# Sample query products moved between gated tiles, page numbers read once, and the order of the SP queue, in a hybrid decoder layer

## The chip, the core and the metric

The kernel runs on one core of a Trainium2 chip. The engines of the core run on their own and meet at semaphores: PE (TensorE) multiplies, with its weight loads (PEld) beside it; DVE (VectorE), ACT (ScalarE) and POOL (GpSimd) work elementwise; SP (SyncE) issues nearly all transfers between HBM and SBUF, one after the other, from a program of its own, and its rows are named SPq in the profile. The metric is the device time of one launch in microseconds (us). Spans and stretches below are counted from the first instruction of the profiled execution.

## The reference, cut to what matters

One layer for 1,024 prompt rows and 32 sample rows (8 requests of 4 tokens). It has a first feed-forward half step, a mixing step, an output projection, a second feed-forward half step and a gated embedding. The change touches the mixing step:

```python
def token_mix(n, prm, q_pos, attend, conv_hist):
    z = n @ prm['w_in']
    cq, ckv_raw, kpe_raw, u = z[..., :o1], z[..., o1:o2], z[..., o2:o3], z[..., o3:]
    q = jnp.einsum('btr,rhd->bthd', rmsnorm(cq, prm['g_q']), prm['w_q_up'])
    q_nope = q[..., :QK_NOPE]
    q_pe = rope(q[..., QK_NOPE:], q_pos)
    ckv = rmsnorm(ckv_raw, prm['g_kv'])
    kpe = rope(kpe_raw, q_pos)
    att = attend(q_nope, q_pe, ckv, kpe)
    v = u[..., :CONV_CH] * jax.nn.sigmoid(u[..., CONV_CH:])     # gated tiles
    ...                                                         # depthwise convolution, 31 taps

def sample_attention(q_nope, q_pe, q_pos, ckv_all, kpe_all, w_uk, w_uv):
    q_abs = jnp.einsum('bthn,rhn->bthr', q_nope, w_uk)
    s = (jnp.einsum('bthr,bsr->bhts', q_abs, ckv_all)
         + jnp.einsum('bthp,bsp->bhts', q_pe, kpe_all))
    ...
    pr = jax.nn.softmax(s, axis=-1).astype(ckv_all.dtype)
    o_lat = jnp.einsum('bhts,bsr->bthr', pr, ckv_all)
    return jnp.einsum('bthr,rhv->bthv', o_lat, w_uv).reshape(B, T, H * V_HEAD)
```

For the prompt rows the keys and values are the 1,024 rows themselves. For the sample rows they are 2,048 cached rows in pages of 128, found through a page table, plus the 4 new ones.

## The kernel before

All 1,056 rows are held as columns, cut into three blocks of 352. The large products are split into three fp32r products (`split_product`, L467 to L471: `wlo` by `n_hi`, `whi` by `n_lo`, `whi` by `n_hi`), so a tile of one 128-wide weight block and 352 columns takes 8 x 3 matmuls. Weight tiles stream from HBM into `raw`, are split by ACT into `whi` and by DVE into `wlo`, and sit in a ring of six.

**The gated tiles** (L581 to L589) are the last part of the input projection. There are 4 channel chunks `c` by 3 row blocks `r`, twelve in all, each with 48 matmuls into two PSUM banks. For each one ACT applies the sigmoid (`gate`, L1003 to L1007) and DVE multiplies (`glu`, L1456 to L1461). Between the first ones PE sums squares for the norms of the latents `cq` and `ckv`.

**The sample queries** (L592 to L616) follow all twelve tiles on PE. 24 products of 128x32 (48 matmul rows in the trace, since an fp32 product is two passes) of `sw` and the sample columns of `cq` go to bank 7. DVE scales them into `qs` (L1500). 32 further products of `qs` with `sw` and `ident` (64 rows) absorb the key up-projection; ACT copies the result into `qabs` (L1044). Between the two, PE transposes the 32 new latent rows, which DVE copies into `ckvnew`, and DVE makes `newT` and the rotary rows of `k` (L1509 to L1511).

**The attention** (L665 to L778) runs over four pairs of heads, `p` = 0 to 3. In each pair PE makes the pair's queries, keys and values out of `cq` and `ckv` with the pair's weights `pw` (`proj`, z = 0 to 7, L671 and L699), then goes through eight blocks of prompt rows: scores (L714), transposes of the probabilities (L729), values (L739), and at the end the reciprocals of the sums (L749). Into it are woven four tiles of sample attention per pair, n = 4p to 4p + 3, sixteen in all, each for 256 cached rows of four requests: `sample_scores(n)` (L629) reads `ttile[n % 2]`, `sample_probs_T(n)` (L643) transposes, `sample_values(n)` (L655) reads `ctile[n % 2]`. The first stands behind z = 2, the second behind the scores of block 1, the third behind block 2 and the fourth in block 5. DVE and POOL share the convolution: POOL takes its chunks in one run once all gated tiles are done, and DVE puts one tap (`convolve`, L1525) behind most of its steps.

**The queue of SP** is written out by hand. After the weight tiles it holds the stores of `kpe` and `ckv`, then, once the last gated tile is multiplied, the loads of `tab` and `pw`, then `load_t(0)`, `load_c(0)`, `load_t(1)`, `load_c(1)`, then five stores of the convolution's state (L375, L377), and then for n = 2 to 15 `load_t(n)`, `load_c(n)`, with the next pair's `pw` behind every fourth. `load_t(n)` may start when `sample_scores(n - 2)` is done, `load_c(n)` when `sample_values(n - 2)` is. Each is eight transfers, one per page and request, and each transfer is preceded by a read of its page number from SBUF into a register:

```python
    def load_t(eng, n):
        if n >= BUFS:
            eng.wait_ge(ss_ready, n - BUFS + 1)
        for j, pg, page in pages_of(eng, n):
            eng.dma_start(ttile[n % BUFS][:, j, :, pg * PAGE:(pg + 1) * PAGE], cacheT[page]).then_inc(t_in[n % BUFS], 16)
```

`pages_of` is a generator, so the read of one page number (L322) and its transfer (L329 or L336) alternate. `ttile1` and `ctile0` lie where `sw` and `qs` lay, `ttile0` where `cs` and `tabs` lay, and `tab`, `pw`, `q`, `k` and `V` lie over `raw` and the ring of weight tiles. PE then goes on to the output projection and the rest of the layer.

Of the kernel before, what the change touches and what calls it, by code (L numbers as in the profile page):

```python
# [6 lines left out]
P = 128  # L7
D_MODEL, SEQ, DEC_B, DEC_T = 1024, 1024, 8, 4
ROWS = SEQ + DEC_B * DEC_T
NRB = 3  # L10
# [112 lines left out]
def program(nc, wstream, pairw, xT, hist, gains, trig, qtrig, strig, samplew, ident_d, tri_d, smask_d, cache, cacheT,  # L123
# [82 lines left out]
    z1 = scope()  # L206
    wuv = sb(z1, "wuv", [P, VC, HEADS * VH])
    z1.close()
    pw = sb(zc, "pw", [P, PW])
    z1 = scope()  # L210
    olatT = sb(z1, "olatT", [P, VC, 2, P])
    z1.close()
    q = sb(zc, "q", [P, 2, SEQ])
# [102 lines left out]
    def pages_of(eng, n):  # L316

        grp, c = divmod(n, TILES)
        for j in range(4):
            for pg in range(PPT):  # L320
                at = (4 * grp + j) * N_PAGES + PPT * c + pg
                yield j, pg, eng.value_load(ptab[0:1, at:at + 1], min_val=0, max_val=cache.shape[0] - 1)  # L322

    def load_t(eng, n):

        if n >= BUFS:
            eng.wait_ge(ss_ready, n - BUFS + 1)
        for j, pg, page in pages_of(eng, n):
            eng.dma_start(ttile[n % BUFS][:, j, :, pg * PAGE:(pg + 1) * PAGE], cacheT[page]).then_inc(t_in[n % BUFS], 16)  # L329

    def load_c(eng, n):

        if n >= BUFS:
            eng.wait_ge(c_used, n - BUFS + 1)
        for j, pg, page in pages_of(eng, n):
            eng.dma_start(ctile[n % BUFS][:, j, pg, :], cache[page]).then_inc(c_in[n % BUFS], 16)  # L336
# [5 lines left out]
    def _(sp):  # L342
# [16 lines left out]
        sp.wait_ge(const_in, 4 * 16)  # L359
        sp.wait_ge(kpe_roped, 1)  # L360
        sp.dma_start(kpeT, kpe[:, :]).then_inc(kpe_out, 16)
        sp.wait_ge(lat_norm, 2 * NRB)
        sp.dma_start(ckvT, ckv[:, :, :]).then_inc(out_state, 16)
        sp.wait_ge(pair_ready, T_FF2)
        sp.dma_start(tab[:, :], qtrig).then_inc(trig_in, 16)
        sp.dma_start(pw[:, :], pairw[0]).then_inc(pw_in, 16)
        sp.wait_ge(qs_ready, 1)
        load_t(sp, 0)
        sp.wait_ge(qa_made, 1)
        load_c(sp, 0)  # L370
        load_t(sp, 1)
        load_c(sp, 1)
        sp.wait_ge(hist_in, 16 * CC)
        sp.wait_ge(pair_free, 2 + T_FF2)
        sp.dma_start(convp, vext[:, :, SEQ:SEQ + HIST]).then_inc(out_state, 16)  # L375
        for c in range(CC):
            sp.dma_start(convs[:, c], vs[:, c, :, DEC_T:DEC_T + HIST]).then_inc(out_state, 16)  # L377
        for n in range(BUFS, LAST + 1):
            load_t(sp, n)
            load_c(sp, n)  # L380
            if n % STEPS == 2:
                p = n // STEPS + 1
                sp.wait_ge(proj_ready, Z_PROJ * p)
                if p < PAIRS:
                    sp.dma_start(pw[:, :], pairw[p]).then_inc(pw_in, 16)
                else:
                    sp.dma_start(wuv[:, :, :], wuv_d).then_inc(wuv_in, 16)
# [78 lines left out]
    def _(pe):  # L466
# [110 lines left out]
        y = Y_LAT  # L577
        for c in range(CC):
            for r in range(NRB):
                t = T_WIN + c * NRB + r  # L580
                pe.wait_ge(w_split, N_WIN + 6 + 2 * c + 2)  # L581
                pe.wait_ge(pair_free, t + 1)
                b = 2 * (t % 2)
                contract(ps[:, b, 0:RB], (2 * c) % RING, r)
                contract(ps[:, b + 1, 0:RB], (2 * c + 1) % RING, r).then_inc(pair_ready, 1)
                x = c * NRB + r - 2
                if 0 <= x < 2 * NRB:
                    row_sum(y, lat_red, x + 1, sqs[:, 0, :])
                    y += 1  # L589


        pe.wait_ge(const_in, 4 * 16)  # L592
        pe.wait_ge(sw_in, 3 * 16)
        pe.wait_ge(lat_norm, 2 * NRB)
        for hd in range(HEADS):
            for c in range(QC):
                w0 = hd % 2 * QC * P + c * P
                last = nc.tensor.matmul(ps[:, 7, hd * NEW:(hd + 1) * NEW], sw[:, hd // 2, w0:w0 + P], cq[:, c, SEQ:ROWS],
                                        start=(c == 0), stop=(c == QC - 1))
        last.then_inc(qs_made, 1)  # L600
        for c in range(VC):
            last = nc.tensor.transpose(ps[0:NEW, 6, c * P:(c + 1) * P], ckv[:, c, SEQ:ROWS],
                                       ident[:, 0:P])
        last.then_inc(new_made, 1)
        pe.wait_ge(qs_ready, 1)
        pe.wait_ge(pair_free, 2 + T_FF2)
        for hd in range(HEADS):
            for c in range(C96 + 1):
                m = ROPE if c == C96 else min(K96, KV_RANK - c * K96)
                out = ps[0:m, hd // 4, (hd % 4 * 4 + c) * NEW:(hd % 4 * 4 + c + 1) * NEW]  # L610
                if c == C96:
                    last = nc.tensor.matmul(out, ident[NOPE:P, P:P + ROPE], qs[NOPE:P, hd, :], start=True, stop=True)
                else:
                    w0 = SW_UKT + hd % 2 * KV_RANK + c * K96
                    last = nc.tensor.matmul(out, sw[0:NOPE, hd // 2, w0:w0 + m], qs[0:NOPE, hd, :], start=True, stop=True)
        last.then_inc(qa_made, 1)  # L616
# [47 lines left out]
        for p in range(PAIRS):  # L664
# [10 lines left out]
            for z in range(4):  # L675
                hh, s0 = z // 2, z % 2 * 512
                if z == 2:
                    pe.wait_ge(new_ready, 1)
                    pe.wait_ge(av_out, QB * p + 1)
# [75 lines left out]
            if p == 0:  # L755
                pe.wait_ge(qabs_ready, 1)
# [118 lines left out]
    def _(act):  # L875
# [147 lines left out]
        lat_squares(0, 0)  # L1023
        for x in range(CC * NRB):
            gate(*divmod(x, NRB))
# [12 lines left out]
        act.wait_ge(qa_made, 1)  # L1038
        for b in range(2):
            for c in range(C96 + 1):  # L1040
                m = ROPE if c == C96 else min(K96, KV_RANK - c * K96)
                dst = qabs[NOPE:K96, 2] if c == C96 else qabs[0:m, c]
                src = ps[0:m, b, :].rearrange("p (h s n) -> p h s n", h=4, s=4)[:, :, c, :]
                last = nc.scalar.activation(dst[:, :, 4 * DEC_T * b:4 * DEC_T * (b + 1)]  # L1044
                                            .rearrange("p b (h t) -> p h b t", h=4),
                                            src.rearrange("p h (b t) -> p h b t", b=DEC_B), ACT.Copy)
        last.then_inc(qabs_ready, 1)

# [10 lines left out]
        def sample_exp(n):  # L1059
# [4 lines left out]
            else:  # L1064
                act.wait_ge(kpe_out, 16)
                act.wait_ge(kpe_ready, 1)
            if n >= 2:
# [178 lines left out]
    def _(ve):  # L1246
# [240 lines left out]
        for x in range(CC * NRB):  # L1487
# [8 lines left out]
            if x == 2 * NRB + 2:  # L1496
                rope_keys()

        ve.wait_ge(qs_made, 1)
        nc.vector.scalar_tensor_tensor(out=qs[:, :, :], in0=ps[:, 7, 0:HEADS * NEW].rearrange("p (h n) -> p h n", h=HEADS),  # L1500
                                       scalar=SCALE, in1=tabs[:, :].rearrange("p (o n) -> p o n", o=1)
                                       .broadcast_to([P, HEADS, NEW]), op0=ALU.mult, op1=ALU.mult).then_inc(qs_ready, 1)
        ve.wait_ge(new_made, 1)
        nc.vector.tensor_copy(ckvnew[:, :], ps[0:NEW, 6, 0:KV_RANK]).then_inc(new_ready, 1)
# [384 lines left out]
```

## Time and profile before

| | us |
|---|---|
| median of 3 runs | 2373.71 (2373.28 to 2376.27) |
| the profiled execution | 2374.75 |
| its span, first to last instruction | 2372.9 |
| PE busy | 2235.9 (94%) |
| DVE, ACT, POOL busy | 1236.1, 599.9, 308.4 |
| mean granted clock of TensorE | 0.975 |

The page's slices show PE at 9 tenths nearly everywhere but in the slices from about 960 to 1340 us, the attention, where it stands at 5 to 9 and the granted clock dips. Stretches of the trace are therefore read one by one. The rows of a timeline give the start, the busy time, the engine, the line, what is written and read, and in brackets how long the engine was idle before and who ended it. A busy PE is not PE at its peak: the column of the granted clock (1.00 is 2.4 GHz, 0.50 is 1.2 GHz) says at which of its two levels it ran.

### The profile page before, as it was taken

The numbers are of one execution on the slowest core, as the hardware profiler recorded it, in microseconds if no ns is written. First come the engines' busy times: TensorE is split into PE (matmuls) and PEld (weight loads), VectorE is DVE, ScalarE is ACT, GpSimd is POOL, SyncE is SP. The second block draws the span as 40 slices with busy tenths as digits, with TensorE's granted clock in tenths as the row PEclk, the third lists the DMA queues.
The fourth block names the chain that finished last, engine by engine and source line by source line (L and its number), as shares of the span: only waits on it lengthen the run. The fifth ranks groups of instructions, "written<-read, shape, count | busy, mean of one in ns | idle before, by whom it ended". The sixth has DMA issues, their size and how long they took to land.

```text
span 2372.9 us, 36251 instructions
## 1 busy us (share of the span) xinstructions
PE 2235.9 (94%) x14234; PEld 2099.8 (88%) x14234; DVE 1236.1 (52%) x1940; ACT 599.9 (25%) x967; POOL 308.4 (13%) x173
## 2 busy tenths in 40 slices
PE   6999999999999999968888899999999999999897
PEld 5999999999999999735544689999999999999796
DVE  7444444444445725457678546544444444445746
ACT  6211111111112314232342433211111111112423
POOL 0000000000000000799995000000000000000000
PEclk9999999999999999878999999999999999999899
DMA  4111111111111330374343311111111111111202
GB/s 149 45 45 44 44 35 53 53 53 37 50 36 36 131 108 9 102 117 123 113 123 114 110 54 54 36 45 44 39 50 53 53 44 45 35 53 36 80 19 73
DMA packets 97113, 150.84 MB, mean 64 GB/s; under 512 B 12113, under 2 KB 73970, under 8 KB 96610
## 3 DMA queue, kind: packets, MB, share of 16 engines
q1 hardware_dynamic: 96098, 140.49, 19.9%
q0 software_dynamic: 928, 9.17, 1.1%
q8 instruction: 58, 0.95, 0.2%
q14 instruction: 29, 0.24, 0.0%
HBM read 139.21 MB, written 10.42 MB: 63 GB/s over the span
## 4 chain that ended last, share of the span: by engine, by line
PE 81%; DVE 10%; ACT 4%; SPq 2%; issue 2%; DMA 1%; DVEq 0%; ACTq 0%
PE ps L469 25%; PE ps L470 24%; PE ps L471 24%; DVE cacc L1525 2%; PE ps L714 2%; PE ps L671 1%; DVE stat L1628 1%; SPq L322 1%; ACT sq L886 1%; SPq L329 1%; PE ps L729 1%; PE ps L739 1%; DVE n L1278 1%; DVE wlo L1251 1%; PE ps L629 1%
## 5 line engine op out<-in xcount | busy, mean ns | idle before, releaser
L469 PE MATMUL ps<-n_hi,wlo 128*128 128x352 f32 x2832 | 922.8, 326 | 21.6 <-DVE wlo L1251 13.7
L471 PE MATMUL ps<-n_hi,whi 128*128 128x352 f32 x2832 | 911.3, 322 | 0.0
L470 PE MATMUL ps<-n_lo,whi 128*128 128x352 f32 x2832 | 910.9, 322 | 0.0
L469 PEld LDWEIGHTS ps<-n_hi,wlo 128*128 128x128 f32 x2832 | 533.9, 189 | 26.1 <-issue 14.4
L470 PEld LDWEIGHTS ps<-n_lo,whi 128*128 128x128 f32 x2832 | 535.4, 189 | 2.0 <-issue 0.2
L471 PEld LDWEIGHTS ps<-n_hi,whi 128*128 128x128 f32 x2832 | 533.7, 188 | 0.0
L469 PE MATMUL ps<-hid_hi,wlo 128*128 128x352 f32 x1104 | 359.7, 326 | 25.1 <-DVE h L1306 12.1
L470 PE MATMUL ps<-hid_lo,whi 128*128 128x352 f32 x1104 | 355.5, 322 | 0.0
L471 PE MATMUL ps<-hid_hi,whi 128*128 128x352 f32 x1104 | 355.4, 322 | 0.0
L1306 DVE SCALAR_TENSOR_TENSOR h<-ps,h 128x352 f32<-128x352 f32 x552 | 273.1, 520 | 153.1 <-PE ps L471 153.1
L1319 DVE TENSOR_TENSOR gact<-ps,rstd 128x352 f32<-128x352 f32 x132 | 69.1, 523 | 530.9 <-PE ps L471 530.9
L917 ACT ACTIVATE gact<-gact 128x352 f32<-128x352 f32 x132 | 65.8, 498 | 1100.2 <-DVE gact L1319 1100.2
L469 PEld LDWEIGHTS ps<-hid_hi,wlo 128*128 128x128 f32 x1104 | 208.5, 189 | 28.9 <-DVE h L1306 13.0
L1251 DVE TENSOR_TENSOR wlo<-raw,whi 128x1024 fp32r<-128x1024 f32 x164 | 197.6, 1219 | 28.3 <-ACT whi L879 28.3
L470 PEld LDWEIGHTS ps<-hid_lo,whi 128*128 128x128 f32 x1104 | 208.9, 189 | 0.3 <-issue 0.2
L471 PEld LDWEIGHTS ps<-hid_hi,whi 128*128 128x128 f32 x1104 | 208.2, 189 | 0.0
L456 POOL TENSOR_TENSOR cacc<-cacc,sqs 128x1024 f32<-128x1024 f32 x74 | 188.1, 2542 | 6.2
L879 ACT ACTIVATE whi<-raw 128x1024 fp32r<-128x1024 f32 x164 | 166.7, 1046 | 63.0 <-DMA raw<-in_wstream 41.9
L1329 DVE TENSOR_TENSOR hid_lo<-prod,hid_hi 128x352 fp32r<-128x352 f32 x132 | 69.3, 525 | 83.8 <-ACT hid_hi L913 83.8
L454 POOL TENSOR_SCALAR sqs<-vext,gain 128x1024 f32<-128x1024 f32 x74 | 109.3, 1477 | 7.3 <-POOL cacc L456 0.2
L430 POOL DMA_DIRECT2D out_yT<-h x1 | 0.6, 565 | 802.7 <-DVE n L1278 802.7
L1525 DVE SCALAR_TENSOR_TENSOR cacc<-vext,gain,cacc 128x1024 f32<-128x1024 f32 x46 | 96.6, 2101 | 0.5
(182 smaller groups left out, 1546.0 us busy)
## 6 DMA issues: line engine op xcount, KB each, us to landing
raw<-in_wstream SPq DMA_DIRECT2D x167, 512.0 KB, 3.6
ttile<-in_cacheT SPq DMA_DIRECT2D x128, 144.0 KB, 2.6
ctile<-in_cache SPq DMA_DIRECT2D x128, 128.0 KB, 2.0
out_yT<-h POOLq DMA_DIRECT2D x1, 4224.0 KB, 13.7
h<-out_yT SPq DMA_DIRECT2D x3, 1408.0 KB, 11.5
out_yT<-n SPq DMA_DIRECT2D x2, 1408.0 KB, 5.7
sw<-in_samplew POOLq DMA_DIRECT2D x1, 2560.0 KB, 10.2
pw<-in_pairw SPq DMA_DIRECT2D x4, 640.0 KB, 4.7
```

What stands on the lines that cost most here:

```text
L454: nc.gpsimd.tensor_scalar(product[:, 0:SEQ], src, w, 1.0, ALU.mult, ALU.mult).then_inc(pool_tap, 1)
L456: nc.gpsimd.tensor_tensor(acc, acc, product[:, 0:SEQ], ALU.add).then_inc(pool_tap, 1)
L469: nc.tensor.matmul(out, w_l, x_h, start=first, stop=False)
L470: nc.tensor.matmul(out, w_h, x_l, start=False, stop=False)
L471: return nc.tensor.matmul(out, w_h, x_h, start=False, stop=last)
L879: nc.scalar.activation(whi[ring][:, :], raw[n % RAW][:, :], ACT.Copy).then_inc(w_hi, 1)
L917: nc.scalar.activation(gact[:, t % 2, :], gact[:, t % 2, :], ACT.Silu).then_inc(act_gate, 1)
L1251: nc.vector.tensor_tensor(wlo[ring][:, :], raw[n % RAW][:, :], whi[ring][:, :].bitcast(f32), ALU.subtract)\
L1306: nc.vector.scalar_tensor_tensor(out=h[:, o, rows(r)], in0=ps[:, 4 + y % 4, 0:RB], scalar=factor, in1=h[:, o, rows(r)], op0=ALU.mult, op1= ...
L1319: nc.vector.tensor_tensor(gact[:, t % 2, :], ps[:, b, 0:RB], rstd[:, r, :], ALU.mult)\
L1329: nc.vector.tensor_tensor(hid_lo[:, f, rows(r)], prod[:, t % 2, :], hid_hi[:, f, rows(r)].bitcast(f32), ALU.subtract).then_inc(hid_ready, 1)
L1525: step.hit(nc.vector.scalar_tensor_tensor(out=acc, in0=src, scalar=w, in1=acc, op0=ALU.mult, op1=ALU.add))
```

## The change

1. **PE**: the sample query products stand behind gated tile (3, 0) and the absorbed products behind gated tile (3, 1), that is ahead of the last two and of the last one of the twelve. The absorbed products go to banks 5 and 6 in place of 0 and 1. The transposes of the new rows stay behind the last tile.
2. **ACT and DVE**: ACT copies `qabs` ahead of the last sigmoid, and DVE scales `qs` behind the multiplication of tile (3, 0).
3. **SP, pages**: the eight page numbers of a tile are read in one go, ahead of the wait, and used for `load_t` and `load_c` both; sixteen are read for the first two tiles.
4. **SP, order**: `tab` and `pw` are loaded as soon as their place in SBUF is free (the arrays in it are laid out anew), `load_t(1)` stands ahead of `load_c(0)`, and the five stores of the convolution's state stand behind `load_c(5)`.

```diff
     def pages_of(eng, n):
         grp, c = divmod(n, TILES)
-        for j in range(4):
-            for pg in range(PPT):
-                at = (4 * grp + j) * N_PAGES + PPT * c + pg
-                yield j, pg, eng.value_load(ptab[0:1, at:at + 1], min_val=0, max_val=cache.shape[0] - 1)
+        return [(j, pg, eng.value_load(ptab[0:1, at:at + 1], min_val=0, max_val=cache.shape[0] - 1))
+                for j in range(4) for pg in range(PPT) for at in [(4 * grp + j) * N_PAGES + PPT * c + pg]]
...
         sp.wait_ge(const_in, 4 * 16)
+        sp.wait_ge(w_split, N_WO)
+        sp.dma_start(tab[:, :], qtrig).then_inc(trig_in, 16)
+        sp.wait_ge(pair_ready, T_WIN + 2 * NRB)
+        sp.dma_start(pw[:, :], pairw[0]).then_inc(pw_in, 16)
+        sp.wait_ge(lat_norm, 2 * NRB)
+        sp.dma_start(ckvT, ckv[:, :, :]).then_inc(out_state, 16)
+        pages = [pages_of(sp, n) for n in range(BUFS)]
         sp.wait_ge(kpe_roped, 1)
         sp.dma_start(kpeT, kpe[:, :]).then_inc(kpe_out, 16)
-        sp.wait_ge(lat_norm, 2 * NRB)
-        sp.dma_start(ckvT, ckv[:, :, :]).then_inc(out_state, 16)
-        sp.wait_ge(pair_ready, T_FF2)
-        sp.dma_start(tab[:, :], qtrig).then_inc(trig_in, 16)
-        sp.dma_start(pw[:, :], pairw[0]).then_inc(pw_in, 16)
         sp.wait_ge(qs_ready, 1)
-        load_t(sp, 0)
+        load_t(sp, 0, pages[0])
         sp.wait_ge(qa_made, 1)
-        load_c(sp, 0)
-        load_t(sp, 1)
-        load_c(sp, 1)
-        sp.wait_ge(hist_in, 16 * CC)
-        sp.wait_ge(pair_free, 2 + T_FF2)
-        sp.dma_start(convp, vext[:, :, SEQ:SEQ + HIST]).then_inc(out_state, 16)
-        for c in range(CC):
-            sp.dma_start(convs[:, c], vs[:, c, :, DEC_T:DEC_T + HIST]).then_inc(out_state, 16)
+        load_t(sp, 1, pages[1])
+        load_c(sp, 0, pages[0])
+        sp.wait_ge(pair_ready, T_WIN + 3 * NRB)
+        load_c(sp, 1, pages[1])
         for n in range(BUFS, LAST + 1):
-            load_t(sp, n)
-            load_c(sp, n)
+            pages = pages_of(sp, n)
+            load_t(sp, n, pages)
+            load_c(sp, n, pages)
+            if n == STEPS + 1:
+                sp.wait_ge(hist_in, 16 * CC)
+                sp.wait_ge(pair_free, 2 + T_FF2)
+                sp.dma_start(convp, vext[:, :, SEQ:SEQ + HIST]).then_inc(out_state, 16)
+                for c in range(CC):
+                    sp.dma_start(convs[:, c], vs[:, c, :, DEC_T:DEC_T + HIST]).then_inc(out_state, 16)
...
+                if (c, r) == (CC - 1, 0):
+                    sample_queries()
+                if (c, r) == (CC - 1, 1):
+                    absorbed_queries()
...
                 hh, s0 = z // 2, z % 2 * 512
+                if z == 1:
+                    pe.wait_ge(qabs_ready, 1)
                 if z == 2:
-                    pe.wait_ge(new_ready, 1)
                     pe.wait_ge(av_out, QB * p + 1)
...
         for x in range(CC * NRB):
+            if x == CC * NRB - 1:
+                take_absorbed()
             gate(*divmod(x, NRB))
...
+            if x == 3 * NRB:
+                ve.wait_ge(qs_made, 1)
+                nc.vector.scalar_tensor_tensor(out=qs[:, :, :], ...).then_inc(qs_ready, 1)
```

Here is PE's order before, from the last matmul of the last gated tile to the first pair projection, with the semaphores that a row waits for (L598 sample queries, L602 transposes, L615 and L612 absorbed products, L671 `proj`):

```order
L471 MATMUL ps<-n_hi,whi 128x352
L598 MATMUL ps<-cq,sw 128x32 [waits lat_norm,sw_in,const_in]
L598 MATMUL ps<-cq,sw 128x32 x23
L602 MATMUL ps<-ident,ckv 32x128 x2
L615 MATMUL ps<-qs,sw 96x32 [waits pair_free,qs_ready]
...
L671 MATMUL ps<-cq,pw 128x512 [waits pw_in]
L671 MATMUL ps<-cq,pw 128x512 x5
L671 MATMUL ps<-cq,pw 128x512 [waits av_out,new_ready]
```

And now, with the three places at which it changed (L474 ends one gated tile, the next L472 begins another; L590, L605 and L628 are what L598, L615 and L602 were, L684 is `proj`):

```order
L474 MATMUL ps<-n_hi,whi 128x352
L590 MATMUL ps<-cq,sw 128x32 [waits lat_norm,sw_in,const_in]
L590 MATMUL ps<-cq,sw 128x32 x23
L472 MATMUL ps<-n_hi,wlo 128x352 [waits pair_free,w_split]
...
L605 MATMUL ps<-qs,sw 96x32 [waits qs_ready]
...
L472 MATMUL ps<-n_hi,wlo 128x352 [waits pair_free,w_split]
...
L628 MATMUL ps<-ident,ckv 32x128 x2
L684 MATMUL ps<-cq,pw 128x512 [waits pw_in]
L684 MATMUL ps<-cq,pw 128x512 x2
L684 MATMUL ps<-cq,pw 128x512 [waits qabs_ready]
```

One wide tile now stands between the query products and the absorbed ones and one between the absorbed ones and the projections; `qabs_ready` is waited for at z = 1 and `new_ready` no longer at z = 2.

SP's queue before, from `tab` on, with one transfer's rows of the page read (`TENSOR_LOAD` and `ISA x2`), the address (`ISA`) and the transfer:

```order
L365 DMA tab<-in_qtrig 128x1024 [waits pair_ready]
L366 DMA pw<-in_pairw 128x1280
L322 TENSOR_LOAD ptab [waits qs_ready]
L322 ISA x2
L329 ISA
L329 DMA ttile<-in_cacheT 96x3x128
...
L322 TENSOR_LOAD ptab [waits qa_made]
L322 ISA x2
L336 ISA
L336 DMA ctile<-in_cache 128x256
```

And now, of the tile n = 2: the eight reads (L319) come first and without a wait, and the sixteen transfers follow in two runs:

```order
L319 TENSOR_LOAD ptab
L319 ISA x2
...
L327 ISA [waits ss_ready]
L327 DMA ttile<-in_cacheT 96x3x128
...
L334 ISA [waits c_used]
L334 DMA ctile<-in_cache 128x256
```

A tile has 8 page reads where it had 16, and the wait for `ss_ready` or `c_used` stands behind them and no longer ahead of them.

## Rows read from the trace of the kernel before

**Rows 1.** Timeline of SP, 880 to 1060 us: start, time over which issued, transfers
```profile
970.29 10.17 SPq L329 DMA_DIRECT2D ttile<-in_cacheT  x8
981.66 8.26 SPq L336 DMA_DIRECT2D ctile<-in_cache  x8
...
1010.66 4.67 SPq L377 DMA_DIRECT2D out_convs<-vs  x4
1016.10 12.33 SPq L329 DMA_DIRECT2D ttile<-in_cacheT  x8
```

**Rows 2.** One transfer's issue on SP: ns, min/median/max, first and last start
```profile
L329 SPq DMA_DIRECT2D ttile<-in_cacheT x128: 572/584/1760, 970.3 to 1293.9; - x128
...
L336 SPq DMA_DIRECT2D ctile<-in_cache x128: 332/333/668, 981.7 to 1302.9; - x128
```

**Rows 3.** Timeline of PE, 962 to 1085 us (idle before it in brackets)
```profile
963.39 5.44 PE L598 MATMUL ps<-cq,sw 128*128 128x32 f32 x48
...
980.23 10.93 PE L671 MATMUL ps<-cq,pw 128*128 128x512 f32 x18
991.09 1.50 PE L629 MATMUL ps<-ttile,qabs 96*32 96x256 f32 x24
...
1031.79 2.79 PE L629 MATMUL ps<-ttile,qabs 96*32 96x256 f32 x24 [14.48 <-DMA ttile<-in_cacheT]
```

**Rows 4.** Stretches: length, busy of PE, PEld, DVE, ACT, POOL, clock, DMA share, GB/s
```profile
963.40:969.00 5.60, 5.60 (x51) 5.37 (x50) 0.72 (x3) 2.53 (x4) 3.86 (x3) 1.00 0.60 214
969.50:980.20 10.70, 10.70 (x64) 9.19 (x64) 6.12 (x9) 0.00 (x0) 10.15 (x7) 0.50 0.29 86
980.20:986.00 5.80, 5.80 (x9) 2.52 (x8) 0.14 (x1) 3.00 (x9) 5.52 (x4) 0.50 0.42 116
...
1031.80:1037.00 5.20, 5.20 (x29) 2.42 (x30) 1.91 (x3) 0.75 (x3) 4.99 (x3) 0.50 0.37 112
```

**Rows 5.** Timeline of ACT, 935 to 1010 us: sigmoids behind gated tiles (3, 0) and (3, 1)
```profile
948.33 0.47 ACT L1003 ACTIVATE vext<-ps 128x352 f32<-128x352 f32 x1 [7.15 <-PE ps L471]
955.96 0.47 ACT L1003 ACTIVATE vext<-ps 128x352 f32<-128x352 f32 x1 [7.16 <-PE ps L471]
```

**Rows 6.** Timeline of PE in pairs 1 to 3: projections' start, first and third sample tile
```profile
1080.31 7.99 PE L671 MATMUL ps<-cq,pw 128*128 128x512 f32 x18
1088.23 1.50 PE L629 MATMUL ps<-ttile,qabs 96*32 96x256 f32 x24
...
1115.36 1.50 PE L629 MATMUL ps<-ttile,qabs 96*32 96x256 f32 x24 [0.24 <-DVE olat L1576]
...
1168.98 7.99 PE L671 MATMUL ps<-cq,pw 128*128 128x512 f32 x18
1176.91 1.50 PE L629 MATMUL ps<-ttile,qabs 96*32 96x256 f32 x24
...
1203.67 1.50 PE L629 MATMUL ps<-ttile,qabs 96*32 96x256 f32 x24
...
1253.61 6.70 PE L671 MATMUL ps<-cq,pw 128*128 128x512 f32 x15
...
1261.54 1.50 PE L629 MATMUL ps<-ttile,qabs 96*32 96x256 f32 x24
...
1290.84 2.73 PE L629 MATMUL ps<-ttile,qabs 96*32 96x256 f32 x24
```

**Rows 7.** Timeline of DVE, 930 to 1015 us: the last copy ahead of pair 0
```profile
974.16 1.52 DVE L1511 COPY k<-kpe 32x1024 f32<-32x1024 f32 x1
```

**Rows 8.** Timeline of POOL: first and last step of its convolution
```profile
964.96 1.19 POOL L450 TENSOR_SCALAR cacc<-vext,gain 128x1024 f32<-128x1024 f32 x1 [131.95 <-DVE vs L1461]
...
1276.90 2.37 POOL L456 TENSOR_TENSOR cacc<-cacc,sqs 128x1024 f32<-128x1024 f32 x1
```

**Rows 9.** The convolution's tap on DVE, 980 to 1275 us, then 1280 to 1345 us
```profile
L1525 DVE SCALAR_TENSOR_TENSOR cacc<-vext,gain,cacc x42: 1272/2036/3300, 989.9 to 1272.6; 128x1024 f32<-128x1024 f32 x42
...
L1525 DVE SCALAR_TENSOR_TENSOR cacc<-vext,gain,cacc x4: 1272/1278/1284, 1279.5 to 1295.6; 128x1024 f32<-128x1024 f32 x4
```

## What I expect, and why

> **What bounds the kernel now.** I read the page's slices first: PE is busy in 94% of the span, so outside the attention only PE work counts, and the change takes none away. The attention is where the slices dip, so I read PE's timeline there. It has one large hole: the third sample tile of pair 0 starts at 1031.79 after 14.48 us without work, ended by the transfer of its `ttile` [rows 3]. SP's timeline says why that transfer is late. The eight transfers of a `ttile` take 10.17 us to issue and those of a `ctile` 8.26 us, one load stands behind the other, the stores of the convolution's state come ahead of the third `ttile`, and so its issue begins at 1016.10 and ends at 1028.4 [rows 1]. PE would have used it from about 1017.3 (1031.79 less 14.48).
>
> The stretches with their clock show a second loss. TensorE keeps 2.4 GHz through the sample queries (963.4 to 969.0), is at 1.2 GHz in the absorbed products, and still in the wide projections from 980.2 to 986.0; behind the hole it is at 1.2 GHz from 1031.8 to 1037.0 [rows 4]. Both times narrow products or nothing preceded.
>
> **The stall in pair 0.** Between the starts of two `ttile` transfers lie (10.17 - 0.58) / 7 = 1.37 us, of `ctile` (8.26 - 0.33) / 7 = 1.13 us [rows 1, 2]. Less the transfers' own issue of 0.58 and 0.33 us, 0.79 and 0.80 us are left for the page read and the address. I give the read 0.7 and the address 0.1. A tile's queue time falls from 8 x (1.37 + 1.13) = 20.0 to 8 x 0.7 + 8 x 0.68 + 8 x 0.43 = 14.5 us. If reads in a run don't overlap their latency this holds, otherwise it is less; neither matters, as the margins show. The absorbed products end near 970 (below). Then `load_t(1)` takes 5.4, `load_c(0)` and `load_c(1)` 3.4 each and the reads of tile 2 5.6 us: SP stands at its next wait at 988. That wait is for the first `sample_scores`, which ends near 990; the third `ttile` is issued by 996 and lands some 3 us later, against a use near 1016. The wait is gone with 17 us to spare. The next `ttile` waits for the second `sample_scores` and 5.6 us of reads, about 1011 to 1016, and is used some 20 us later. The five stores (some 6 us of queue: the four of L377 take 4.67 and end right ahead of 1016.1 [rows 1]) now stand behind `load_c(5)`, which itself waits for the fourth `sample_values`, about 1054; behind them is queued `load_t(6)`, which may not start before pair 1's first `sample_scores` near 1075 anyway and is used near 1103. I cost their move at nothing. Who waits for `load_t(1)` ahead of `load_c(0)`: the first `sample_values` needs `ctile0` 12 us after the first scores, near 1001, and it is issued by 979. `tab` and `pw` are asked for well before their use in both kernels, so that their move gains nothing on the path.
>
> What takes the stall's place? I compare the same stretches of other pairs [rows 3, 6]. From first to third `sample_scores`: 40.7 us in pair 0 (991.09 to 1031.79), 27.1, 26.8 and 29.3 in pairs 1, 2 and 3. I take their mean, 27.7, rather than 40.7 - 14.5 = 26.2, for the DVE reason below. From there to the next pair's first projection: 48.5 in pair 0 (to 1080.31), 53.6 in pair 1, 49.9 in pair 2. Pair 0 has here both the slow clock's return (5.2 us at half speed, 2.6 lost) and a DVE that had caught up in the hole. Without the hole both vanish, so I take the mean of the three, 50.7. Pair 0 from its first scores on: 27.7 + 50.7 = 78.4 in place of 89.2, a gain of **10.8**.
>
> **The moved products.** Gated tile (3, 0) ends at 948.33, the next 7.6 us later [rows 5]. From 948.3 to the first scores at 991.09 are 42.8 us. No product is removed. At full clock the pieces are: sample queries 5.4 [rows 3], two wide tiles 15.2, absorbed products half of 10.9, that is 5.4 (64 rows, all at 0.50 [rows 4]), transposes 0.4, and z = 0 to 2 at full clock 7.9 (1080.31 to 1088.23 [rows 6]): 34.3 us. Before, a slow clock from 969.3 to 986.2 adds half of 16.9, which makes 42.8: the sum closes.
>
> The absorbed products are bounded below by their weight loads. By the Trainium skill (TensorE: Matmul & The Clock Gate, LDWEIGHTS) a load takes a time given by its columns alone; a head has 96 + 96 + 64 + 32 columns, twice, against 128 per row of the sample queries, which would give 4.1 us and a sum 1.3 us lower. No row here has them at full clock. From above, the sample queries' spacing of 0.113 us times 64 gives 7.3 us. I keep 5.4, the half, between the two.
>
> After, the clock will see narrow work twice, with a wide tile behind each. The clock before fell 5.7 to 6 us after the last wide matmul, and came back some 6 us after wide work resumed [rows 3, 4]. The sample queries last 5.4 and the absorbed ones 5.4, so I expect a fall at about the end of each and 6 us of each wide tile at half speed: 2 x 3.0. From 948.3 then 34.3 + 6.0 = 40.3, the first scores at 988.6 in place of 991.1, a gain of **2.5**. The projections of pair 0 run at full clock at last, but the two tiles pay most of that back. ACT's copy of `qabs` (1.8 us) lies under the last tile, and DVE's `qs` under tile (3, 1); the wait for `qabs_ready` at z = 1 is met 9 us ahead.
>
> DVE's copies of `newT` and `k`, which begin behind the transposes and end at 975.7 [rows 7], lay under the absorbed products and now come behind the last tile's multiplication and the transposes, under z = 0 to 2. Counted from the sample transposes they take about 6.5 us of these 8.3; the first scores wait for `kpe_ready` and just don't lose. The first taps and `sample_max(0)` are queued behind them, and DVE arrives about 2 us later relative to PE. That is why I took 27.7 and not 26.2 above.
>
> **POOL later.** Its convolution starts when the last gated tile is multiplied, 964.96 before [rows 8], now 17 us later (948.3 + 5.4 + 10.6 + 5.4 + 10.6 = 980.3 for the tile's end), and ends at 1296 in place of 1279. The attention then ends near 1326 (1253.61 plus at least 84 us for a pair, less 12), so nothing waits for POOL. But DVE's taps take 2.04 us at the median while POOL works and 1.28 us without it [rows 9], and four taps of pair 3 were in the quiet stretch: 4 x 0.76 = 3.0 us more DVE time, most of it beside waits. I charge **1.0** us, between 0 and 3.
> The Trainium skill (GPSIMD Engine Reference, Specifications) says that GpSimd shares its SBUF interface with VectorE and contends with instructions of two SBUF inputs. The trace agrees for this tap; the rule speaks against the change.
>
> **Sum.** 10.8 + 2.5 - 1.0 = 12.3 us. The span goes from 2372.9 to 2360.6, the execution (1.85 more) to 2362.4. The profiled execution lay 1.04 above the median of its three runs, so the median is 2361.4.
>
> **Rivals.**
> A. The clock holds. If tiles of 7.6 us around 5.4 us of narrow work keep it at 2.4 GHz, the 6.0 us are saved too: 2355.4. For it: it held through all of the sample queries. Against: it was at half speed right behind them.
> B. The absorbed products still run at 1.2 GHz from their start, because the clock is not yet back from the sample queries: 5.4 more, 2366.8. Against: tile (3, 1) lasts longer than the 6 us.
> C. DVE becomes the bound of pair 0: it enters late, and ACT's exponentials wait for its maxima. The worst stretches of other pairs, 29.3 and 53.6, give 82.9 in place of 78.4: 2365.9.
> D. Slower: the clock does not come back within the short wide tiles. Then both take 15.2 in place of 7.6 (9.2 more than my 6.0), the absorbed products 10.9 (5.4 more) and z = 0 to 2 10.9 (3.0 more): 17.6 more, 2379. It decides against the change from 12.3 us of such losses on. Against: twice wide work had the clock back after 5 to 6 us [rows 4].
> E. The third `ttile` is late all the same, for a reason not in the queue: the hole moves by the 2.5 us only, about 2371.
>
> **How the numbers follow.** Forecast 0.55 (2357.5 to 2365.4), A 0.16, B 0.09, C 0.14, D 0.02, E 0.04. The outer bounds are 2351 (no fall, pair 0 at 26.8 + 48.5, POOL free) and 2373 (B and C, POOL at 3.0); 8 in 10 lie between 2353 and 2368.5. 0.2%, 4.7 us, is about what a measurement here can tell. Faster than 2369.0: forecast, A and nearly all of B and C, 0.93; same 0.05; slower 0.02.
>
> **What would show it.** In the new trace: no wait of PE for `ttile` in pair 0; runs of eight transfers near 5.4 and 3.4 us; about 78 us from pair 0's first scores to pair 1's projections; a clock of 0.50 in two spells of some 6 us in tiles (3, 1) and (3, 2) and 1.00 in z = 0 to 2; the first scores near 988.6; POOL's end near 1296. The forecast is wrong if the clock's spells differ in number or length, or if pair 0 finds a wait for DVE longer than in the other pairs.

## The result

The changed kernel is slower: 2381.22 us at the median of six runs (2377.45 to 2383.71) against 2372.7 us (2370.49 to 2376.27) for the kernel before. The ratio is 1.0034, with a 95% interval of 1.0022 to 1.0047. The profiled execution is its fastest, 2377.45 us with a span of 2375.4, so the sums below are made on 2.5 us more span than before, not on the 8.5 of the medians; the other 6 us no profile here shows.

The stall that I had aimed at is gone. This is PE's timeline of the changed kernel at the end of the gated tiles and in pair 0 (L590 sample queries, L605 absorbed products, L684 projections, L642 `sample_scores`, L763 reciprocals):

```profile
947.64 6.79 PE L590 MATMUL ps<-cq,sw 128*128 128x32 f32 x48
963.98 0.75 PE L605 MATMUL ps<-qs,sw 64*96 64x32 f32 x6
...
981.55 7.89 PE L684 MATMUL ps<-cq,pw 128*128 128x512 f32 x18
989.37 1.50 PE L642 MATMUL ps<-ttile,qabs 96*32 96x256 f32 x24
...
1017.43 2.61 PE L642 MATMUL ps<-ttile,qabs 96*32 96x256 f32 x24
...
1065.26 7.99 PE L684 MATMUL ps<-cq,pw 128*128 128x512 f32 x18
```

The first scores start at 989.37 (991.09 before), the third `sample_scores` follows 28.1 us later without a wait (40.7 before [rows 3]), and pair 1 begins at 1065.26 in place of 1080.31 [rows 6], 15 us ahead. The loss comes at the other end. Pair 3 begins at 1240.47, still 13 us ahead, and then:

```profile
1240.47 7.99 PE L684 MATMUL ps<-cq,pw 128*128 128x512 f32 x18
...
1280.48 1.12 PE L753 MATMUL ps<-PT,V 128*64 128x128 f32 x8 [6.91 <-ACT PT L1123]
...
1295.27 4.56 PE L728 MATMUL ps<-k,q 128*128 128x512 f32 x8 [9.48 <-ACT pr L1136]
...
1306.15 4.54 PE L728 MATMUL ps<-k,q 128*128 128x512 f32 x8 [4.27 <-ACT pr L1136]
...
1340.61 1.95 PE L763 MATMUL ps<-ident,precs 128*64 128x128 f32 x32
```

PE waits 6.9, 9.5 and 4.3 us for ACT. Pair 3 takes 102.1 us (1240.47 to 1342.56) where it took 86.1 (1253.61 [rows 6] to 1339.7, the end of the same reciprocals). ACT in turn waited for the maxima of DVE; this is the list of who waited for whom in that stretch, the changed kernel's first line and then the same one of the kernel before (1253 to 1340 us):

```profile
ACT pr L1136 <- DVE stat L1646: 46.1, 13, 14.0
```

```profile
ACT pr L1119 <- DVE stat L1628: 30.7, 13, 5.4
```

And DVE was busy. Its timeline in the changed kernel at the second of four sample convolutions (32 sample columns of one channel chunk: four products `terms_s`, a sum over taps, a bias), with POOL's steps of the same time behind it:

```profile
1283.50 6.53 DVE L1558 TENSOR_TENSOR terms_s<-vs,gain 128x248 f32<-128x248 f32 x4
1290.06 1.19 DVE L1563 TENSOR_REDUCE cacc<-terms_s 128x32 f32<-128x992 f32 x1
1291.29 2.19 DVE L1565 TENSOR_SCALAR cacc<-cacc,gain 128x32 f32<-128x32 f32 x1
```

```profile
1282.59 3.20 POOL L459 TENSOR_TENSOR cacc<-cacc,sqs 128x1024 f32<-128x1024 f32 x1
1285.89 1.41 POOL L457 TENSOR_SCALAR sqs<-vext,gain 128x1024 f32<-128x1024 f32 x1
1287.38 2.38 POOL L459 TENSOR_TENSOR cacc<-cacc,sqs 128x1024 f32<-128x1024 f32 x1
...
1299.62 2.40 POOL L459 TENSOR_TENSOR cacc<-cacc,sqs 128x1024 f32<-128x1024 f32 x1
```

In the kernel before, the first of the four groups began at about the same time and ran alone, since POOL had ended at 1279.3 [rows 8]:

```profile
1283.38 1.39 DVE L1540 TENSOR_TENSOR terms_s<-vs,gain 128x248 f32<-128x248 f32 x4
1284.80 1.19 DVE L1545 TENSOR_REDUCE cacc<-terms_s 128x32 f32<-128x992 f32 x1
1286.02 0.24 DVE L1547 TENSOR_SCALAR cacc<-cacc,gain 128x32 f32<-128x32 f32 x1
```

Before, POOL's end and the first sample convolution lay 4.1 us apart. The change moved POOL 23 us later (its end 1302.0; it starts 17.9 us later, at 982.90, and its steps take 4.8 us more in all) and this part of pair 3 13 us earlier, so three of the four groups met POOL. Their excess over 1.39 and 0.24 us is 4.9, 7.1 and 3.0 us (the timeline has 4.39 + 2.11, 6.53 + 2.19, and 4.39 + 0.24), together 15.0 of the 16.0 us by which the pair is longer. That is added up from single steps, but the engine's total agrees: DVE is busy for 78.7 us of pair 3 in place of 62.1. TensorE's granted clock is lower over the pair too, 0.85 in place of 0.96, and PE is busy for 74.7 us in place of 70.2; how much of that lies on the path is not told apart. One line for each kernel gives it at a glance, all sixteen products, min/median/max in ns, changed kernel first:

```profile
L1558 DVE TENSOR_TENSOR terms_s<-vs,gain x16: 403/416/2575, 1269.9 to 1307.7; 128x248 f32<-128x248 f32 x16
```

```profile
L1540 DVE TENSOR_TENSOR terms_s<-vs,gain x16: 405/408/414, 1283.4 to 1303.3; 128x248 f32<-128x248 f32 x16
```

The sum closes: start of the sample queries' stage 0.6 us earlier, to the first scores 1.1 gained, pair 0 from there 75.9 in place of 89.2, 13.3 gained; pairs 1 and 2 175.2 in place of 173.3, 1.9 lost; pair 3 16.0 lost; behind it 0.3 gained. That makes the 2.5 us more, within rounding.

### The profile page after: what moved, and what is told of

The parts are those of the page before. It is cut to its first block, busy times and chain, and to the rows that moved or that the text cites. A ratio compares the mean times of both kernels' runs of the same rounds, so it can differ in the third digit from the quotient of the medians.

```text
span 2375.4 us, 35863 instructions
## 1 busy us (share of the span) xinstructions
PE 2239.8 (94%) x14234; PEld 2104.0 (89%) x14234; DVE 1256.6 (53%) x1940; ACT 600.0 (25%) x967; POOL 313.2 (13%) x173
## 4 chain that ended last, share of the span: by engine, by line
PE 80%; DVE 13%; ACT 4%; issue 2%; DMA 1%; DVEq 0%; SPq 0%; ACTq 0%
PE ps L472 25%; PE ps L473 24%; PE ps L474 24%; DVE cacc L1543 3%; PE ps L684 1%; DVE stat L1646 1%; PE ps L728 1%; ACT sq L898 1%; PE ps L743 1%; DVE terms_s L1558 1%; DVE n L1295 1%; DVE wlo L1268 1%; PE ps L826 1%; PE ps L753 1%; DVE rstd L1287 1%
## 5 line engine op out<-in xcount | busy, mean ns | idle before, releaser
L472 PE MATMUL ps<-n_hi,wlo 128*128 128x352 f32 x2832 | 924.3, 326 | 21.4 <-DVE wlo L1268 13.9
L474 PE MATMUL ps<-n_hi,whi 128*128 128x352 f32 x2832 | 912.5, 322 | 0.0
L472 PEld LDWEIGHTS ps<-n_hi,wlo 128*128 128x128 f32 x2832 | 535.1, 189 | 25.6 <-issue 14.3
L474 PEld LDWEIGHTS ps<-n_hi,whi 128*128 128x128 f32 x2832 | 535.0, 189 | 0.0
L472 PE MATMUL ps<-hid_hi,wlo 128*128 128x352 f32 x1104 | 361.2, 327 | 22.0 <-DVE h L1323 12.2
L474 PE MATMUL ps<-hid_hi,whi 128*128 128x352 f32 x1104 | 356.2, 323 | 0.0
L472 PEld LDWEIGHTS ps<-hid_hi,wlo 128*128 128x128 f32 x1104 | 209.3, 190 | 25.4 <-DVE h L1323 13.0
L474 PEld LDWEIGHTS ps<-hid_hi,whi 128*128 128x128 f32 x1104 | 209.2, 189 | 0.0
L459 POOL TENSOR_TENSOR cacc<-cacc,sqs 128x1024 f32<-128x1024 f32 x74 | 193.0, 2608 | 6.2
L891 ACT ACTIVATE whi<-raw 128x1024 fp32r<-128x1024 f32 x164 | 166.7, 1046 | 62.1 <-DMA raw<-in_wstream 41.1
L728 PE MATMUL ps<-k,q 128*128 128x512 f32 (+3 forms) x192 | 80.3, 564 | 24.1 <-ACT pr L1136 24.1
## 6 DMA issues: line engine op xcount, KB each, us to landing
h<-out_yT SPq DMA_DIRECT2D x3, 1408.0 KB, 11.5
```

Of the source, the lines that this page charges most:

```text
L459: nc.gpsimd.tensor_tensor(acc, acc, product[:, 0:SEQ], ALU.add).then_inc(pool_tap, 1)
L472: nc.tensor.matmul(out, w_l, x_h, start=first, stop=False)
L474: return nc.tensor.matmul(out, w_h, x_h, start=False, stop=last)
L728: last = nc.tensor.matmul(psf[:, s0 + c:s0 + e], q[:, hh, i * P:(i + 1) * P], k[:, hh, c:e], start=True, stop=True)
L891: nc.scalar.activation(whi[ring][:, :], raw[n % RAW][:, :], ACT.Copy).then_inc(w_hi, 1)
```

## The experiments

The theory: **POOL's steps stretch DVE's sample convolution where they meet in pair 3**. The rival: the loss comes from the new SP queue, or from something else in pair 3. Each median in the runs below was taken on one chip beside the kernel before, whose own median lay between 2372.7 and 2374.9 in these sets, and the ratio is to that one; the stages are read from the profiled executions (pair 0 from its first projection to pair 1's, pair 3 to the end of its reciprocals).

| kernel | median | ratio, 95% interval | pair 0 | pairs 1, 2 | pair 3 | POOL ends |
|---|---|---|---|---|---|---|
| before | 2372.7 | 1 | 100.1 | 173.3 | 86.1 | 1279 |
| changed | 2381.2 | 1.0034 [1.0022, 1.0047] | 83.7 | 175.2 | 102.1 | 1302 |
| SP part alone | 2369.0 | 0.9980 [0.9971, 0.9990] | 85.2 | 167.9 | 98.5 | 1279 |
| products alone | 2391.7 | 1.0077 [1.0060, 1.0094] | 105.5 | 175.5 | 86.0 | 1297 |
| before, POOL late | 2382.9 | 1.0036 [1.0024, 1.0049] | 100.4 | 176.9 | 92.4 | 1296 |
| changed, POOL short | 2362.8 | 0.9948 [0.9931, 0.9964] | 85.3 | 178.3 | 84.1 | 1271 |
| changed, late sample convolutions | 2365.6 | 0.9970 [0.9958, 0.9981] | 83.7 | 175.2 | 91.2 | 1301 |
| before, late sample convolutions | 2370.8 | 0.9990 [0.9981, 1.0000] | 103.2 | 170.5 | 82.2 | 1277 |
| SP part, late sample convolutions | 2362.4 | 0.9949 [0.9932, 0.9966] | 85.0 | 176.7 | 89.6 | 1281 |
| state stores moved alone | 2370.0 | 0.9989 [0.9979, 0.9999] | 90.1 | 170.7 | 95.7 | 1282 |

The stages of one profile are not exact. Two of these kernels were profiled a second time, for the last experiment. The changed one with late sample convolutions gave 83.7 and 88.6 us for pair 0, 175.2 and 170.5 for pairs 1 and 2, and 91.2 both times for pair 3. The SP part with late sample convolutions gave 85.0 and 88.8, 176.7 and 178.5, and 89.6 and 80.9. So a difference of 5 us in pair 0 or of 9 us in pair 3 can be that of two executions of one kernel, and what a kernel is worth is told from medians. What the profiles do show is which steps of DVE were stretched.

**POOL late, and nothing else.** The kernel before with

```diff
         pool.wait_ge(pair_free, 2 + T_FF2)
+        pool.wait_ge(qa_made, 1)
```

> The kernel before, with one wait added: POOL starts its convolution only when the absorbed products are done (980 in place of 965). Nothing else differs. Theory: POOL ends near 1294 to 1298 and meets two or three of the sample convolutions of pair 3: 6 to 12 us slower than before, 2379 to 2385 us, terms_s steps over 1 us in the trace. Rival (POOL's end doesn't matter): within 2 us of before, 2372 to 2375 us.

It is 9 us slower at the median. Its profile shows one group stretched, as in the changed kernel, under POOL's last steps (DVE, then the line of POOL that ends last):

```profile
1287.93 4.40 DVE L1541 TENSOR_TENSOR terms_s<-vs,gain 128x248 f32<-128x248 f32 x4
1292.37 1.19 DVE L1546 TENSOR_REDUCE cacc<-terms_s 128x32 f32<-128x992 f32 x1
1293.59 2.11 DVE L1548 TENSOR_SCALAR cacc<-cacc,gain 128x32 f32<-128x32 f32 x1
```

```profile
1293.32 2.34 POOL L457 TENSOR_TENSOR cacc<-cacc,sqs 128x1024 f32<-128x1024 f32 x1
```

I had expected two or three groups; one met POOL. The size at the median agrees; the pair is 6.3 us longer, of which the group accounts for 4.9, and DVE is busy in it for 6.3 us more than before (68.4 in place of 62.1). A later POOL alone makes the kernel slower by as much as the whole change did, with SP, PE and ACT untouched.

**POOL short.** The changed kernel without 8 of POOL's 14 taps on chunk 2 (that part of the result is left out):

```diff
-            for x in range(first, TAPS):
+            for x in range(first, TAPS - 8 * (c == SHARED)):
```

> The changed kernel with the last 8 of POOL's 14 taps on channel chunk 2 left out (that part of the convolution is not computed), so that POOL ends some 31 us earlier, near 1270. All else is the changed kernel. Theory: the sample convolutions of pair 3 run alone, pair 3 takes 84 to 88 us in place of 102, and the time is 2360 to 2364 us. Rival (not POOL): pair 3 keeps its 102 us and the time stays at 2377 to 2384 us.

All sixteen products take 406 to 417 ns and pair 3 84.1 us in place of 102.1; the median falls by 18 us. POOL still works for the first 21.6 us of pair 3 (1249.4 to 1271.0) in place of 61.5 (1240.5 to 1302.0), and ends before the first sample convolution at 1278.8. So the last 31 us of its work hold the loss. The rival on the SP queue falls with this run: its queue is the changed one.

**Each part alone.** The SP part on the kernel before, and the moved products on the kernel before.

> Only the SP part of the change on the kernel before: page numbers read once per tile and ahead, tab and pw loaded early, load_t(1) ahead of load_c(0), state stores behind load_c(5). PE, ACT and DVE keep their old order, so POOL starts its convolution at 965 and ends near 1279. Theory (POOL's steps stretch DVE's sample convolution, the terms_s steps, where they meet in pair 3): the 14.5 us wait for ttile is gone, pair 3 starts near 1241, POOL still works for the first 9 us of its blocks 1 and 2 and one or two sample convolutions are stretched by 3 to 6 us: 2363 to 2369 us, terms_s steps up to 2.5 us in the first of four groups and 0.41 in the others. Rival (the loss comes from the SP queue itself, its runs of transfers or the moved state stores): pair 3 is as long as in the changed kernel, 102 us, and the time stays near 2378.

2369.0: the gain of 15 us in pair 0 arrives, and pair 3, which begins earlier against a POOL that ends where it did, gives 12 us back, so the size was at my upper bound. One group is stretched:

```profile
1267.65 4.37 DVE L1543 TENSOR_TENSOR terms_s<-vs,gain 128x248 f32<-128x248 f32 x4
1272.06 1.19 DVE L1548 TENSOR_REDUCE cacc<-terms_s 128x32 f32<-128x992 f32 x1
1273.28 2.10 DVE L1550 TENSOR_SCALAR cacc<-cacc,gain 128x32 f32<-128x32 f32 x1
```

This group explains 4.8 of the 12.4 us. DVE is busy for 12.3 us more than before in the pair, and the rest is in its other steps with operands in SBUF. POOL works for the first 47 us of this pair in place of 26: the nine taps take 20.7 us in place of 18.2, one step on `at_raw` (`n_lo`, 128x1024, L1593) 3.4 in place of 1.2, and the small steps on `stat` (L1567 and L1577, four each) 6.0 in place of 3.3. So the meeting with POOL carries the loss here too, but the sample convolution is less than half of it.

> Only the products moved between the last gated tiles (with their waits, ACT's and DVE's steps); the SP queue as before. Theory: the wait for ttile in pair 0 stays (14.5 us), pair 3 starts 2 to 3 us earlier than before, POOL starts 17 us later and ends near 1296 to 1300, so that two or three of the four sample convolutions meet it: 6 to 14 us lost in pair 3, 2376 to 2385 us. Rival (SP queue is the cause): 2370 to 2372 us, with pair 3 at 86 us.

It is 18 us slower than before, more than I expected, and for another reason. PE's timeline has three waits for transfers in it, where the kernel before had one of 14.5 us (L681 projections, L639 `sample_scores`):

```profile
985.58 10.92 PE L681 MATMUL ps<-cq,pw 128*128 128x512 f32 x18 [5.13 <-DMA pw<-in_pairw]
1014.43 1.89 PE L639 MATMUL ps<-ttile,qabs 96*32 96x256 f32 x24 [3.99 <-DMA ttile<-in_cacheT]
1041.11 2.79 PE L639 MATMUL ps<-ttile,qabs 96*32 96x256 f32 x24 [14.58 <-DMA ttile<-in_cacheT]
```

In the old queue `pw` is asked for only when the last gated tile is multiplied, which used to be covered by 16 us of sample products and is now followed by 0.4 us of transposes. I had costed the early load of `pw` at no gain; with the products moved it is worth 5.1 us. These waits pushed pair 3 to 1266.56, so far back that POOL's end at 1296.9 lies just ahead of its first sample convolution at 1297.9: 86.0 us, no collision, against my expectation.

**Late sample convolutions.** In pair 3, DVE's program:

```diff
-                if p == PAIRS - 1 and 1 <= i <= CC:
-                    convolve_sample(i - 1)
+                if p == PAIRS - 1 and i >= 5:
+                    convolve_sample(i - 5)
...
             nc.vector.reciprocal(precs[:, :], psums[:, :]).then_inc(rec_ready, 1)
+            if p == PAIRS - 1:
+                convolve_sample(3)
```

> The changed kernel with the four sample convolutions moved, in DVE's program, from blocks 1 to 4 of pair 3 to blocks 5, 6 and 7 and to the place behind the reciprocals, all of them past POOL's end near 1300. The same work is done. Theory (sample convolutions meeting POOL's steps cost the 16 us): pair 3 takes 84 to 90 us and the time is 2361 to 2366 us, terms_s steps 0.41 us each. Rival (POOL slows pair 3 by way of the ordinary steps of DVE, the taps and masks, too): pair 3 keeps more than 92 us, 2370 us or more.

> The kernel before with the four sample convolutions moved to the same later places (blocks 5 to 7 of pair 3 and behind the reciprocals). Theory: before, they already ran alone (0.41 us a step), so moving them gives back only what DVE's 2.8 us each held up in blocks 1 to 4, where PE waited for DVE by way of ACT: 0 to 5 us, 2369 to 2374 us. Rival (it is the place in the block sequence and not POOL that costs): as much gain here as in the changed kernel, 10 us or more, 2363 us.

> SP part of the change alone, with the sample convolutions moved late as well. Theory: POOL ends near 1277, pair 3 starts near 1232 to 1240 and takes 83 to 88 us: 2355 to 2361 us, faster than both kernels. Against the changed kernel with the same move this tells what the moved products are worth: by my forecast they gain 2.5 us, so this one should be 1 to 3 us slower than that one; if the two spells at 1.2 GHz and POOL's later start eat that, it is equal or faster.

The changed kernel goes from 2381.2 to 2365.6, the kernel before only from 2372.7 to 2370.8, its interval ending at no change. So the place in the block sequence costs little and the meeting with POOL costs much. The medians of both lie where I had expected them. Pair 3 of the changed kernel takes 91.2 us, above my theory's 90 and below the rival's 92: the first group still starts at 1298.0 and its four products take 4.20 us beside POOL's last steps. The SP part with the same move, 2362.4, is above my 2355 to 2361, and 3.1 us faster than the changed kernel with it, where my forecast would have had it 1 to 3 us slower.

**Only the state stores moved**, behind `load_c(5)`, in the kernel before.

> The kernel before with only the five stores of the convolution's state moved behind load_c(5); page reads and all other orders as before. Theory: the third ttile is issued from 1010 on in place of 1016, PE's wait in pair 0 falls from 14.5 to 7 to 9 us, pair 3 starts 6 to 8 us earlier and its first sample convolution meets POOL's last steps: 2366 to 2371 us. Rival (the stores' many small packets are what delays the ttile, not the queue's order): the wait goes altogether, 2360 to 2364 us.

```profile
1023.22 2.79 PE L630 MATMUL ps<-ttile,qabs 96*32 96x256 f32 x24 [5.16 <-DMA ttile<-in_cacheT]
```

The wait falls from 14.5 to 5.2 us, by 9.3, which is more than the 6 us of queue that the stores took, and the median, 2370.0, lies in my range. The two timelines of SP say where the rest came from. The third `ttile` is issued from 1011.1 on in place of 1016.1, its eight transfers take 10.1 us to issue in place of 12.3, and PE starts on it 2.0 us behind the end of the issue in place of 3.4. So with the stores ahead of it, it was later and also slower (its slowest landing was 11.5 us). The rival has a part in it, but the wait did not go altogether. Pair 3 takes 9.6 us more than before; here too one group is stretched (4.37 us), and the `n_lo` step takes 3.4 us.

**What are the moved products worth?** The last runs compared three kernels in one go, all with the late sample convolutions.

> The changed kernel with the late sample convolutions once more, in more rounds and on the same chip as the next one, to compare the two directly. Theory: 2363 to 2367 us.

> SP part alone with the late sample convolutions once more. It differs from the kernel run ahead of it only in where the sample query and absorbed products stand. Theory (they gain only 1.1 us ahead of pair 0, since the clock falls twice, and POOL's 17 us later end takes more than that back in pair 3): 1 to 5 us faster than that one, 2360 to 2364 us. Rival (the products gain what I had forecast, 2.5 us): 2 to 3 us slower than that one.

> As the one ahead of it, with three taps of channel chunk 2 given from POOL to DVE (20 taps of DVE in place of 17), which fills idle steps of DVE's in pair 3. POOL ends some 12 us earlier, near 1266. Theory (every step of pair 3 that no longer meets POOL gains, at 0.8 us for a tap): 1 to 4 us faster, 2357 to 2362 us. Rival (DVE's three extra taps of 1.3 us cost what is gained): equal within 1 us.

With both parts 2367.8 (0.9971 [0.9961, 0.9982]), with the SP part alone 2361.8 (0.9941 [0.9927, 0.9955]): moving the products costs some 6 us even here (3.1 in the earlier set), where I had forecast a gain of 2.5. Giving three taps of POOL's to DVE (20 in place of 17) brought 2364.1 (0.9958 [0.9943, 0.9972]), no gain beside the 2361.8, against my 1 to 4 us; it is 2.3 us slower, where the rival had said equal within 1 us, and no run shows why. To see whether POOL's later start explains the 6 us, it was imposed on the SP part alone, with the wait of the first experiment:

> SP part alone with the late sample convolutions, and POOL made to start only when the absorbed products are done (near 981 in place of 966), as late as in the changed kernel. The products stand where they stood before. It asks why moving them costs 6 us beside the late sample convolutions. Theory (POOL's later end): 2365 to 2369 us, as the kernel with both parts. Rival (the second spell at the low clock and DVE's later entry into pair 0): 2361 to 2363 us, as the kernel without this wait.

It stays at 2362.6 (0.9948 [0.9935, 0.9962]), as the rival said: POOL's later start alone does not cost the 6 us, and my theory falls here. The rival's first half, the second spell at the low clock, does not explain them either. That spell lies ahead of the first scores, and these start at 989.7 and 990.7 in the two profiles with the products moved and between 990.6 and 992.2 in the four without. What is lost is lost behind them. DVE's copies, which enter pair 0 later, are the one cause that I can name, and no run tests it; it stays open.

The fastest kernel with the whole result is the SP part with the late sample convolutions: 0.9941 of the kernel before in one set of runs and 0.9949 in the other, faster than both kernels.

## Why the prediction was wrong, point by point

- **The stall in pair 0: right.** No wait for `ttile` is left, and 989.4 to 1065.3 is 75.9 us where I had 78.4. The late entry of DVE that I allowed for shows in one wait of PE for DVE there, of 0.6 us. The same order of work, profiled in the two kernels with late sample convolutions, took 75.9 and 80.8 us, so being nearer to 76 than to 78 says little. SP's timeline of the changed kernel shows the third `ttile` issued 26 us ahead of its use, and a run of eight at 6.3 and 3.9 us, where I had 5.4 and 3.4:

```profile
991.17 6.28 SPq L327 DMA_DIRECT2D ttile<-in_cacheT  x8
1002.22 3.94 SPq L334 DMA_DIRECT2D ctile<-in_cache  x8
```

- **The clock: right in kind.** Two spells at 1.2 GHz, each of some 6.7 us, and 2.4 GHz in z = 0 to 2. Both began within the narrow work and not at its end: at about 951.5, 3.9 us into the sample queries, which took 6.6 us for it in place of 5.4, and at about 968.6, 4.6 us into the absorbed products, which took 8.1 us in all. The stretches of the changed kernel, granted clock in the third column from the end:

```profile
952.50:958.00 5.50, 5.50 (x23) 5.50 (x23) 0.42 (x1) 0.00 (x0) 0.00 (x0) 0.50 0.11 32
959.00:968.00 9.00, 9.00 (x70) 8.25 (x68) 0.52 (x1) 0.46 (x1) 0.00 (x0) 1.00 0.34 92
968.50:975.00 6.50, 6.50 (x34) 5.92 (x33) 0.00 (x0) 1.72 (x8) 0.00 (x0) 0.50 0.13 38
```

- **The absorbed products: mis-sized.** At 2.4 GHz a head of them takes 0.86 us (963.98 to 964.84), not the half of 1.36, so eight would take 6.9 and not 5.4 us. The estimate by the Trainium skill's rule that a weight load goes by its columns (TensorE: Matmul & The Clock Gate, LDWEIGHTS), 4.1, was further off; the upper bound, the spacing of the sample queries, was near. From the start of the sample queries to the first scores, 1.1 us were gained and not 2.5.
- **POOL later: the step that failed.** I charged 1.0 us, between 0 and 3, from one row: the tap's median with and without POOL. I did ask who is slowed when POOL works into pair 3, and answered with the instruction I had a row for. The 16 products, 4 sums and 4 bias steps of the sample convolution were never looked at. They stood 4.1 us behind POOL's end, and each of the small ones can lose 1 to 2 us where a tap loses 0.8: 0.41 became up to 2.58 us. The term measured 16 us in the profile of pair 3; by the medians, shortening POOL gave the changed kernel 18 us, and moving the sample convolutions gave it 15.6 us against 1.9 in the kernel before. It also sits on the path, since the maxima of the next block, which ACT and PE wait for, are queued right behind them on DVE.
- **The rivals.** None of mine was it. The slower one, D, had the wrong mechanism, the clock. The Trainium skill's rule that I cited (GPSIMD Engine Reference, Specifications) was the right one against this change, and my price for it was wrong. The trace agrees with it in detail: products whose operands both lie in SBUF were stretched, and the sum over taps with its one operand kept 1.19 us with and without POOL. Another page of the Trainium skill (Trainium Architecture — The Big Picture, What this means for kernel authors) calls the port pair an exclusive lock and not a split of bandwidth; steps of 0.41 us that last up to 2.58 beside steps of POOL's of 2.4 fit that, but no run here tells a lock from another cause.
- **`tab` and `pw` at no gain**: right for the queue alone, wrong beside the moved products, where the old place of `pw` costs 5.1 us.

## What to carry to other kernels

When an edit brings one engine's stretch forward or pushes another's back, list every instruction that the two now have beside each other, above all the small ones with two SBUF operands on DVE beside a run of GpSimd, and look at the distance that kept them apart before: here 4 us guarded 16. A row for the commonest instruction does not price the rest. And an edit that pays in a pair (the queue of SP) is worth trying without the one that only moves work (the products): alone it gave 0.2% where both together lost 0.3%, and with the sample convolutions moved out of the way it gave 0.5 to 0.6% where both together gave 0.3%.

## What the runs showed of the hardware that I had not expected

- A DVE product of 128x248 with both operands in SBUF takes 0.41 us alone and up to 2.58 us beside POOL's elementwise steps of 128x1024; a bias step of 128x32 goes from 0.24 to 2.19 us. A DVE sum over 128x992 of one SBUF operand stays at 1.19 us in both kernels, and the mask step (`ps`, `tri`, 128x128, one operand in PSUM) keeps 0.28 to 0.30 us in all 64 of its executions, beside POOL and behind it.
- In the changed kernel PE's granted clock went to 0.50 (1.2 GHz) within both runs of 32-column products, stayed there for 6.7 and 6.6 us, and came back to 1.00 (2.4 GHz) in the wide tile behind each, though PE was busy all the while.
- Two profiled executions of one kernel differ by up to 8.7 us in pair 3 (89.6 and 80.9), 4.9 in pair 0 and 4.7 in pairs 1 and 2, while their times differ by 5.4 us or less (2367.6 and 2362.2, 2365.6 and 2367.1); an effect of a few us in one stage of a single profile is hidden by that.
